# Reordered instruction streams at five stage boundaries of a two-block transformer kernel

## What is computed

```python
proj = rmsnorm(h, norm_gain[l]) @ w_in[l]            # x2 layers
h = h + concat([do, fo]) @ w_out[l]
x = x + 0.5 * swiglu(rms_norm(x, ffn1_norm), wg, wu, wd)
x = x + concat([o_nsa, o_sb]) @ w_out_2
x = x + memory_cross_attention(rms_norm(x, mem_x_norm), rms_norm(mem, mem_kv_norm), ...)
x = x + 0.5 * swiglu(rms_norm(x, ffn2_norm), wg, wu, wd)
```

## Time and profile before

| | us |
|---|---|
| runs | 1987.02, 1977.88, 1977.92; median 1977.92 |
| profiled execution | 1985.47, its span 1983.7 |
| TensorE busy | 1921.9 (97%) |
| VectorE, ScalarE, GpSimd busy | 779.8, 707.4, 712.1 |
| mean granted TensorE clock | 0.987 |
| moved by DMA | 144.2 MB, 73 GB/s |

### The profile page before, as it was taken

One profiled execution on the slowest core, in us unless ns is written; L12 is line 12 of the kernel. 1 busy time (PEld: TensorE's weight loads), 2 busy tenths in 40 slices (PEclk: granted clock), 3 DMA queues, 4 the chain that ended last, 5 costly groups with the idle time before them and its releaser, 6 DMA issues.

```text
span 1983.7 us, 26722 instructions
## 1 busy us (share of the span) xinstructions
PE 1921.9 (97%) x10968; PEld 1646.1 (83%) x10968; DVE 779.8 (39%) x1308; ACT 707.4 (36%) x1328; POOL 712.1 (36%) x343
## 2 busy tenths in 40 slices
PE   7999989999998999999999999899999999999999
PEld 6999878989987897888888878799867878888887
DVE  5433373464326536441112255536676451111001
ACT  3112355321125544223222223435565552222211
POOL 4333201353331014555554423320003435555443
PEclk9999899999999999999999999979999999999999
DMA  4222200122221003222223233110002212222223
GB/s 142 86 79 82 65 1 1 54 85 86 78 85 41 1 13 100 87 94 96 96 91 98 92 109 118 65 43 2 1 1 97 95 54 96 96 96 96 91 88 108
DMA packets 40585, 144.22 MB, mean 73 GB/s; under 512 B 4624, under 2 KB 4880, under 8 KB 40336
## 3 DMA queue, kind: packets, MB, share of 16 engines
q1 hardware_dynamic: 40464, 142.51, 21.6%
HBM read 140.40 MB, written 2.10 MB: 72 GB/s over the span
## 4 chain that ended last, share of the span: by engine, by line
PE 88%; DVE 6%; ACT 3%; issue 1%; DMA 1%; POOL 0%; SPq 0%; DVEq 0%; ACTq 0%
PE ps L354 22%; PE ps L355 22%; PE ps L356 22%; PE ps L871 6%; PE ps L852 5%; PE ps L861 3%; PE ps L2030 1%; DMA raw<-wstream 1%; PE ps L2013 1%; DVE xl L425 1%; PE ps L2002 1%; PE ps L500 1%; PE ps L989 1%; ACT wh L342 1%; PE ps L1774 1%
## 5 line engine op out<-in xcount | busy, mean ns | idle before, releaser
L350 POOL TENSOR_TENSOR wl<-raw,wh 128x1024 fp32r<-128x1024 f32 (+2 forms) x254 | 603.6, 2376 | 838.9 <-ACT wh L342 838.9
L354 PE MATMUL ps<-xh,wh 128*128 128x512 f32 (+3 forms) x1752 | 626.4, 358 | 20.3 <-POOL wl L350 12.5
L355 PE MATMUL ps<-xl,wh 128*128 128x512 f32 (+3 forms) x1752 | 619.9, 354 | 0.0
L356 PE MATMUL ps<-xh,wl 128*128 128x512 f32 (+3 forms) x1752 | 618.1, 353 | 0.0
L342 ACT ACTIVATE wh<-raw 128x1024 fp32r<-128x1024 f32 (+2 forms) x254 | 266.0, 1047 | 969.8 <-PE ps L356 903.1
L354 PEld LDWEIGHTS ps<-xh,wh 128*128 128x128 f32 x1752 | 330.8, 189 | 75.4 <-issue 18.4
L355 PEld LDWEIGHTS ps<-xl,wh 128*128 128x128 f32 x1752 | 331.1, 189 | 49.0 <-issue 1.7
L356 PEld LDWEIGHTS ps<-xh,wl 128*128 128x128 f32 x1752 | 331.5, 189 | 47.2
L1116 POOL TENSOR_TENSOR xl<-xb,xh 128x512 fp32r<-128x512 f32 (+1 forms) x22 | 26.1, 1186 | 339.9 <-ACT xh L1025 339.9
L355 PE MATMUL ps<-aL,wh 128*128 128x512 f32 x352 | 139.4, 396 | 0.0
L356 PE MATMUL ps<-aH,wl 128*128 128x512 f32 x352 | 139.2, 396 | 0.0
(11 more groups left out here) (346 smaller groups left out, 2666.4 us busy)
## 6 DMA issues: line engine op xcount, KB each, us to landing
raw<-wstream SPq DMA_DIRECT2D x236, 512.0 KB, 3.5
raw<-wstream SPq DMA_DIRECT2D x16, 384.0 KB, 3.0
raw<-wstream SPq DMA_DIRECT2D x10, 528.0 KB, 3.6
h<-xT SPq DMA_DIRECT2D x4, 528.0 KB, 6.6
out<-h SPq DMA_DIRECT2D x8, 256.0 KB, 3.9
hm<-memT SPq DMA_DIRECT2D x1, 1024.0 KB, 4.8
cst<-const SPq DMA_DIRECT2D x1, 720.5 KB, 9.5
cst<-const SPq DMA_DIRECT2D x1, 320.0 KB, 4.0
```

The lines of the kernel that those rows point to most:

```text
L350: e.tensor_tensor(wl[p % 2][:, 0:n], raw[c % 2][:, 0:n], wh[p % 2][:, 0:n].bitcast(F32), ALU.subtract).then_inc(*w_lo(p))
L354: e.matmul(o, w_h, x_h, start=start, stop=False)
L355: e.matmul(o, w_h, x_l, start=False, stop=False)
L356: return e.matmul(o, w_l, x_h, start=False, stop=stop)
```

## The change

First tiles: the three kinds of product of tiles 0 and 1 run one kind after another, over all pieces, and the norm of the layer stands between the second and third kind of tile 1. TensorE begins with 22 matmuls on a zeroed tile. split_hi(1) stands after piece 7 of xh. GpSimd clears xm first, and QB and QA after split_lo(1). The rest is the same work in another place of an engine's program.

```diff
+        def early_tile(e, on, key, o, n, x_hi_of, x_lo_of, src, between=None):
...
+            on.wait_ge(*w_hi[p])
+            for j, (w, t, ready) in enumerate(((hh, th, x_hi_of), (ll, th, x_hi_of), (hh, tl, x_lo_of))):
+                if w is ll:
+                    on.wait_ge(*w_lo[p])
+                for k in range(KT):
+                    on.wait_ge(*ready(k))
+                    for i in range(2):
+                        r = e.matmul(o[:, i, :], w[:, 128 * k:128 * k + 128], t[:, k, i * m:i * m + m],
+                                     start=j == 0 and k == 0, stop=j == 2 and k == KT - 1)
+                if j == 1 and between:
+                    between()
+            r.then_inc(*tile(*key))
@@ proj_pe @@
-                feature_tile(e, on, key, out_of(key, n), n, c0, normed(st), X[l])
-                if j == 0:
+                if l == 0 and j < 2:
+                    early_tile(e, on, key, out_of(key, n), n, lambda k: x_hi[st, k], lambda k: v_lo[st, k], X[l],
+                               (lambda: norm_pe(e, on, st, L, 2, pair(st), SUMMED(st))) if j else None)
+                else:
+                    feature_tile(e, on, key, out_of(key, n), n, c0, normed(st), X[l])
+                if l and j == 0:
                     norm_pe(e, on, st, L, 2, pair(st), SUMMED(st))
@@ proj_act @@
+            if l == 0:
+                split_hi(e, on, p + 2)
             norm_act_scale(e, on, st, L, 2, bank[st], 1, rst[:, 0:L])
             for j, (kind, c) in enumerate(FEATS):
-                split_hi(e, on, p + j + 2)
                 if l == 0 and j == 10:
...
+                if j or l:
+                    split_hi(e, on, p + j + 2)
@@ proj_dve: the copies into xm (L665 to L669) move from ahead of the loop to here @@
                 if j == 3:
                     turned_scale_dve(e, on, st, 5, rT)
+                    ...
+                    e.tensor_copy(xm[:, :, 0:16], X[l][0][:, :, 0:16].bitcast(F32))
+                    e.tensor_copy(xm[:, :, 32:48], X[l][1][:, :, 0:16].bitcast(F32)).then_inc(*v_one("meta rows", l))
@@ proj_pool @@
-            for q in range(PART["dq", l, 0], PART["gate", l, 7] + 1):
+            for q in range(PART["dq", l, 0] + 2 * (l == 0), PART["gate", l, 7] + 1):
@@ ffn_act (final_act no longer stands ahead of it) @@
+            split_hi(e, on, PART[st + "g", 0] + 2)
+            if st == "ffn1":
+                final_act(e, on)
+                split_hi(e, on, PART[st + "u", 0] + 2)
+            else:
+                split_hi(e, on, PART[st + "u", 0] + 2)
+                norm_act_scale(e, on, st, T, 1, bank[st], 1, rst[:, 0:T])
             for f in range(FT):
-                split_hi(e, on, PART[st + "g", f] + 2)
-                if st == "ffn2" and f == 0:
-                    norm_act_scale(e, on, st, T, 1, bank[st], 1, rst[:, 0:T])
+                if f:
+                    split_hi(e, on, PART[st + "g", f] + 2)
...
-                split_hi(e, on, PART[st + "u", f] + 2)
+                if f:
+                    split_hi(e, on, PART[st + "u", f] + 2)
@@ head_rope_dve ends after the add; the low parts are head_low_dve @@
-        def hooks_dve(e, on, j):
+        def hooks_dve(e, on, j, between=None):
             for what, key in hooks(j):
-                (head_norm_dve if what == "norm" else head_rope_dve)(e, on, key)
+                if what == "norm":
+                    head_norm_dve(e, on, key)
+                else:
+                    head_rope_dve(e, on, key)
+                    if between:
+                        between()
+                    head_low_dve(e, on, key)
+        KEYS_AT = (10, 11, 14)
@@ mix_pe, mix_act: keys at KEYS_AT instead of 10, 11, 12 @@
@@ mix_dve @@
                 if j == 9:
-                    hooks_dve(e, on, j)
-                if key in NORMED:
+                    hooks_dve(e, on, j, lambda: head_out_dve(e, on, key, r))
+                elif key in NORMED:
                     head_out_dve(e, on, key, r)
...
-                    hooks_dve(e, on, j)
-                    if j < 13:
-                        keys_dve(e, on, j - 10)
-                    if v and half == 0:
+                    def three_out():
                         for i in range(3):
                             values_out(v, i)
+                    hooks_dve(e, on, j, three_out if j == 12 else None)
+                    if j in KEYS_AT[:2]:
+                        keys_dve(e, on, KEYS_AT.index(j))
+                    if j == 14:
+                        three_out()
+                    if j == KEYS_AT[2]:
+                        keys_dve(e, on, 2)
@@ memory_pe and memory_act @@
-                if c == 5:
+                if c == 6:
@@ memory_act @@
-                    if m % 4 == 3:
-                        split_hi(e, on, PART["mo", half] + 2)
+                    if m == 3:
+                        split_hi(e, on, PART["mo", 0] + 2)
                     gained_hi(e, on, "ffn2", m, h[:, m, M:L], P_("g_ffn2", m, m + 1), xh[:, m, M:L], v_out["mo", m])
+            split_hi(e, on, PART["mo", 1] + 2)
@@ tensor @@
+            on.wait_ge(*v_one["warm"])
+            on.wait_ge(*v_one["psum", 7])
+            for _ in range(22):
+                e.matmul(PS[:, 512 * 7:512 * 7 + 128], tmpn[:, 0, 0:128], tmpn[:, 0, 0:128], start=True, stop=True)
@@ scalar @@
-                if k in (1, 3):
-                    split_hi(e, on, k // 2)
+                if k in (1, 7):
+                    split_hi(e, on, k // 6)
@@ vector @@
-            for k in range(8):
+            e.memset(tmpn[:, 0, 0:128], 0.0).then_inc(*v_one("warm"))
+            for k in (7, 0, 1, 2, 3, 4, 5, 6):
@@ gpsimd @@
+            e.memset(xm[:, :, :].bitcast(F32), 0.0).then_inc(*p_one("meta rows"))
             split_lo(e, on, 0)
-            e.memset(QA[:, :, :], 0.0).then_inc(*p_one("clear", 0, 0))
             split_lo(e, on, 1)
             e.memset(QB[:, :, :], 0.0).then_inc(*p_one("clear", 0, 1))
-            e.memset(xm[:, :, :].bitcast(F32), 0.0).then_inc(*p_one("meta rows"))
+            e.memset(QA[:, :, :], 0.0).then_inc(*p_one("clear", 0, 0))
+            split_lo(e, on, 2)
+            split_lo(e, on, 3)
```

More of the change, by code:

```diff
@@ L356, in mm3 @@
             return e.matmul(o, w_l, x_h, start=False, stop=stop)
+        def early_tile(e, on, key, o, n, x_hi_of, x_lo_of, src, between=None):
+            p = PART[key]
+            hh, ll = wh[p % 2], wl[p % 2]
+            th, tl = src
+            m = n // 2
+            on.wait_ge(*w_hi[p])
[10 more added lines that the diff above has]
+            r.then_inc(*tile(*key))
         def feature_tile(e, on, key, o, n, c0, x, src=None, nk=KT, col=None, last=True):
@@ L664, in proj_dve @@
             QB = Q_of[l][1]
[L665 to L669, removed]
             on.wait_ge(*a_one[st, "scale"])
@@ L698, in proj_dve @@
                     turned_scale_dve(e, on, st, 5, rT)
+                    on.wait_ge(*x_hi[st, KT - 1])
+                    on.wait_ge(*v_lo[st, KT - 1])
+                    on.wait_ge(*p_one["meta rows"])
+                    e.tensor_copy(xm[:, :, 0:16], X[l][0][:, :, 0:16].bitcast(F32))
+                    e.tensor_copy(xm[:, :, 32:48], X[l][1][:, :, 0:16].bitcast(F32)).then_inc(*v_one("meta rows", l))
             if l == 0:
@@ L1584, in head_rope_dve, with head_low_dve @@
             e.tensor_tensor(u, u, v, ALU.add).then_inc(*roped(*key, "add"))
+        def head_low_dve(e, on, key):
+            u = scratch[:, 0, 0:head_cols(key)[0]]
             for g, (p0, p1, highs, lows) in enumerate(highs_lows(key)):
@@ L1632, in mix_pe @@
                     hooks_pe(e, on, j)
-                    if j < 13:
-                        keys_pe(e, on, j - 10)
+                    if j in KEYS_AT:
+                        keys_pe(e, on, KEYS_AT.index(j))
             for c in range(4):
@@ L1669, in mix_act @@
                     hooks_act(e, on, j)
-                    if j < 13:
-                        keys_act(e, on, j - 10)
+                    if j in KEYS_AT:
+                        keys_act(e, on, KEYS_AT.index(j))
                     if half == 0:
@@ L2309, in scalar @@
                 wout_act(e, on, l)
-            final_act(e, on)
             ffn_act(e, on, "ffn1")
@@ L2392, in program @@
             for k in range(8):
-                freed[k] = [(v_one["psum", k])]
+                freed[k] = [v_one["psum", k]]
             f(count, count)
```

## The result

The changed kernel takes 1957.61 us (median of 6 runs, 1955.54 to 1967.35), the kernel before 1978.56 (median of six runs: five from 1977.88 to 1987.02, and a disturbed one of 3154.39, which the ratio leaves out). The ratio is 0.9892, 95% interval 0.9871 to 0.9912: 1.1% faster, 17 to 26 us. Forecast were 1958.6 us and 0.90 for faster.

The account below looks back on a forecast made before the run. TensorE, busy 97% of the span, was taken as the bound, so only its idle and half-clock time counted. The terms 5.9 + 1.3 + 1.3 + 8.9 + 1.3 + 0.6 = 19.3 us took 1977.9 to 1958.6, own range 1953 to 1963.

Parts of the forecast that it names:

- The view: Whole kernel: TensorE is busy 97% of the span; only its 62 us of idle time and its half-clock time count.
- The start: First tiles: tile 2 starts at 25.6 instead of 31.51, -5.9 us, with bounds -2.5 and -6.5.
- what is late next is GpSimd: First tiles: GpSimd's second split ends at 25.5 after split 1 and two clears, so tile 2 starts at 25.6.
- Lambda, ffn1, memkv: Layer 0's lambda exponents, ffn1's third part and memkv's sums: moved steps remove one TensorE stall each, -1.3 us each.
- Mixing: Mixing stage: earlier evictions and later key rotation remove waits and clock drops, -8.9 us, bounds 5.8 and 9.5.
- ffn2: End of memory block and ffn2's start: reordered copies give -0.6 us, between +0.6 and -2.3.
- The 7.55 us between profile and median: Profiled run against median: a stretch at clock 0.55 in 1320 to 1340 us explains the gap, costing about 6.3 us.
- (1): NSA's start: the half-clock stretch falls into most runs of the new kernel, 1966.1 us; chance 0.18.
- (2): Start: the clock falls again after the zeros or clears push GpSimd's split 2, 3.4 us less gain, 1962.0; chance 0.13.
- (4): Mixing moves only pass the wait on; 4 of 9 us stay, half of start's and ffn2's too, 1968 to 1970; chance 0.06.
- (5): NSA attention stays at half clock beyond the first stretch, so the kernel is slower, up to some 2008; chance 0.02.
- (3): 220 to 240 us: another phase may spare the low clock of 0.71, 5 us or so, giving 1953; chance 0.07.

Follow-up runs that it names:

- e2: The changed kernel without the 22 matmuls on zeros; 1957.34 us.
- e1: The kernel before, unchanged, profiled once more; 1978.81 us, with a span of 1977.0.
- e9: The changed kernel with the weight copies around layer 0's lambda exponents and in ffn_act in their old places; 1961.50 us.
- e10: The kernel before with nothing but the edits of the mixing stage; 1968.54 us (five runs), ratio 0.9959.
- e8: The changed kernel with the weight copy of mo's second half ahead of the last xh piece, as before; 1964.41 us.
- e6: The changed kernel with the three value evictions of turn 12 of the mixing stage behind the low parts again; 1959.62 us.
- e4: The changed kernel with split_hi(1) after piece 3 of xh, as before; 1961.20 us.
- e5: The changed kernel with nk1's eviction behind norm and low parts, as before; 1960.95 us.
- e7: The changed kernel with the third key step of the mixing stage at turn 12 again; 1959.56 us.

## Why the prediction was right, point by point

- **The view.** That only TensorE's idle and half-clock time counts held. e2, which has no zeros to blur the count, has 1909.7 us of busy and 45.8 of idle time, and e1, the kernel before without the stretch, 1913.8 and 63.2: 17.4 us are idle time and 4.1 are clock. (The 20.6 us of idle time between the first two profiles equal the 20.6 between the spans of e1 and the changed kernel by chance.) VectorE's, ScalarE's and GpSimd's busy time moved by 9 us at most.
- **The start** (-5.9, measured -5.69). The chain of sums was timed to 0.2 and 0.35 us (norm forecast 20.6, ran at 20.81; rope 24.7, ran at 25.05). The step "what is late next is GpSimd" was only half right: its split ended at 25.53, but rope ended after it and was the later one. The prediction gave the zeros no price of their own, only the rival that the clock falls behind them (3.4 us); e2, expected to show 2.5 us or more, shows 0. They hide a ramp that the wait for the sums hides anyway. What carries the gain are the order of products and the copy's place, and they overlap (3.5 and 3.65).
- **Lambda, ffn1, memkv** (-1.3 each): 1.27, 1.27, 1.34 by the brackets, 1.47, 1.44 and 1.59 from start to start, shown by the stalls gone and, for the first two, by their return in e9. memkv's was not brought back into the changed kernel; it is there (1.35) in e10, which has the old place.
- **Mixing** (-8.9, measured -9.21): all three waits and both drops of the clock. The parts were forecast as 4.9, 3.4 and 1.0 (less 0.4 at the norm), and undoing them costs 4.29, 3.58 and 0.97. The clock's share is the loosest term: against e1 the same change is worth 10.28, beyond the bound of 9.5.
- **ffn2** (-0.6, measured -0.91). From start to start the second tile came 0.09 us sooner (6.91 to 6.82; forecast 0.1), the third took 0.71 longer (7.07 to 7.78; forecast 0.7), and the fourth 1.53 less (7.21 to 5.68; forecast 1.2, which was the idle time in brackets). The two moves lumped here have opposite signs, as the sum had it: ffn_act's order gains, and the memory end's move loses 0.52, where I had -0.1 + 0.7 = +0.6 of loss. That the adds would move behind the split and carry the delay on is what e8 shows.
- **The 7.55 us between profile and median.** The reading that the stretch near 1320 explains it held in kind. Its price of 6.3 was too low: the estimate took the window 1320 to 1340 alone, while the clock is down from 1315 on (0.74 in 1315 to 1320), and from ks to mk the stretch costs 8.03 us.
- **Rivals.** (1), the stretch in most runs, did not come true: by its time it is in one of six runs of the changed kernel, and by the trace in one variant of eleven (e8). No run shows that the change acts on it, so that the median escaped it is in part luck. (2) did not arise at the start, (4) and (5) neither. (3) did not arise: the clock is 0.74 in 220 to 240, as against 0.71.

## What to carry to other kernels

Where one engine is busy 97% of the time, list its stalls with their releasers, and ask for each what the releasing engine did just before: here it was often a weight copy, waiting for something else, ahead of a short urgent step (start, lambda, ffn1, ffn2), and in the mixing stage VectorE's low parts, waiting for ScalarE, ahead of an eviction. Follow each moved step one stage further, since a copy moved behind the critical step can be late for the next one: the same 1.10 us came back under another name. Judge changes of a microsecond by stretches between two matmuls in the traces, because one half-clock stretch moves the total by eight, and measure them from start to start: the idle time in brackets was 0.17 to 0.34 us short here.

## What the runs showed that was not expected

- Waits of TensorE of 2.12, 3.62 and 3.69 us (e6, e4, e5) were each followed by some microseconds at half clock, and the price was then above the wait: 3.58 for a wait of 2.12 (e6), 3.65 where 2.3 was expected (e4). A wait of 1.05 cost 0.97 and no clock (e7).
- Matmuls on zeros ahead of the work did not hold the clock over a wait of 3.62 us (0.64 and 0.68 behind it, e4), and were not needed to raise it (e2). The 22 took between 6.49 us (e4) and 8.10 us (the changed kernel).
- The block between VectorE and GpSimd goes both ways. In the before profile, e1 and e4 VectorE stood idle when GpSimd's second split of the start began, and the split took 2.36 or 2.37 us; in the other eleven traces VectorE was at an xl piece then, and the split took 2.71 to 2.99 us. In the changed kernel that piece ends 0.73 us behind the split's start, and the split is 0.63 longer.
